# Rows of an expert's slots picked out of the resident residual by TensorE instead of gathered from DRAM

## The chip, the cores and the metric

The program runs on one core of a Trainium2 chip. A core has five engines, each with its own instruction stream: TensorE (PE, with a separate queue of weight loads, PEld), VectorE (DVE), ScalarE (ACT), GpSimd (POOL) and SyncE (SP, which here only issues DMAs). Sixteen DMA engines move data between DRAM and the on-chip memories SBUF (128 partitions) and PSUM (8 banks, written by TensorE). Engines wait for each other and for DMAs on semaphores.

The metric is the device time of one execution in microseconds; lower is better.

## The reference

One decoder layer on 264 tokens (256 of a prompt, 8 of a sample) with D_MODEL 2048, all in float32: token mixing, a mixture of experts, a gated per-layer embedding, a final norm. The change lies in the mixture of experts:

```python
x = x + hier_moe(rmsnorm(x, g_ffn), w_router_g, ..., w_gate, w_up, w_down)

# hier_moe: top-1 of 4 groups, then top-2 of the group's 8 experts; 32 experts of width 512
g_idx = argmax(g_logits); top_l, top_i = top_k(e_logits[g_idx], 2)
expert = g_idx * 8 + top_i
# rows sorted by expert, and for each expert e, with xb its tokens' rows of rmsnorm(x):
(silu(xb @ w_gate[e]) * (xb @ w_up[e])) @ w_down[e]
# the rows go back to their tokens, times their weights
```

Each of the three weights of an expert is 4 MB, so the experts read 32 x 12 MB, about 403 MB, from DRAM.

## The kernel before

**Stages.** The kernel projects, runs attention and the mLSTM, projects out, routes (`route`), runs the experts (`experts`) and ends in `tail_stage`. Each engine's stream is written out by hand; the order inside an engine is the order of the code.

**Tokens.** The residual after token mixing stays in SBUF in `x_res` [128, 3, 2048]: tokens lie on partitions, in three tiles (`TILES`) of 128, 128 and 8 tokens.

**Slots.** Every expert has 32 slots (`SLOTS`), one per token that chose it (more tokens would cause a second pass, `body(p)` with p > 0, which these inputs don't run). `route` computes which token has which rank in its expert: `rank` [128, 6], then `hot` [128, 6, 32], a one-hot row of the slot for each token (six: two choices times three tiles). `choice` holds for each token and expert the token's row number. TensorE multiplies them (`slot_table`, 24 matmuls in bank 4), and `slot_index` turns the table into row indices `idx` with an index out of bounds for an empty slot.

**Layout of an expert's input.** A row of 2048 is cut into four quarters of 512. Partition 32a + s of the tile `xe` [128, 512] holds quarter a of slot s.

**How `xe` was filled.** ACT multiplied all rows by 1/rms (`L1530`) and wrote them to a DRAM tensor `ffn_rows` by three DMAs (`L1532`). POOL gathered from it with an indirect DMA of 128 rows of 2 KB (`gather_rows`, L1905): the first with `first_rows`, the later ones, one per expert, with the index column copied to `gi` (L1899). The gather for expert e + 1 was issued after the matmuls of `x_turn` for expert e had read `xe`. The last one (column 32) has only indices out of bounds. After the expert POOL scatters the results `yq` to `expert_rows` with another indirect DMA of 128 rows (L1914).

**An expert on TensorE** (`expert`, L1852): two halves of the gate product and two of the up product (`project`, 8 matmuls each, L1827), a fold of the gate (`folded(0)`) between the two up halves, the fold of the up product, the down product in two halves (L1847), and `x_turn` (L1807), which turns `xe` of the next expert; DVE copies it to `xT` (`x_copy`, L1762). In the first four experts (`PEELED`) the products of `ple_project` follow.

**Weights.** They come in chunks of 2 MB: gate, up and down of an expert are two each. Six chunks fit in the ring (`raw` and `more`). SP issues the next chunk into a place as soon as TensorE has used the old one (`chunk_used`, L1683). In the routing stage SP loads the six chunks of expert 0 (L1418), and the two gate chunks of expert 1 into other free memory (`extra`, L1448). Those waited until the first gather had landed. Then SP waits for `xs_clear` from POOL (two memsets that follow the first gather, L1929 and L1930), issues four small loads (L1722), loads the flag of a second pass (L1665), and begins the ring.

Of the kernel before, what the change touches and what calls it, by code (L numbers as in the profile page):

```python
# [22 lines left out]
F32 = mybir.dt.float32  # L23
# [1246 lines left out]
def one_hot(core, dve, rt, shared, rank):  # L1270

    core.nc.vector.tensor_tensor(rt["hot"][:], rt["slot"][:].rearrange("p (o s) -> p o s", o=1).to_broadcast([P, 6, SLOTS]),
                                 rank.rearrange("p (m o) -> p m o", o=1).to_broadcast([P, 6, SLOTS]), ALU.is_equal
                                 ).then_inc(shared["hot_ready"], 1)


def slot_index(core, dve, rt, shared, p):
# [7 lines left out]
    if isinstance(p, int):  # L1285
        V.tensor_tensor(rt["first_rows"][:], rt["wide"][:, 0, 0:1], rt["none"][:, 0, 0:1], ALU.add)
# [36 lines left out]
def route(core, w, part, mixT, rt, rows, shared, ctx):  # L1323
# [30 lines left out]
    shifted = slice(32, 32 + NS)  # L1354
    sample_rows = core.x_res[shifted, 2, :]
    extra = [[oT[:].rearrange("p k t -> p (k t)")[:, 0:4096]], [core.gain_row[:], space[:, 0:2048]]]
    names = ("r_xT r_added r_ss r_wr_clear r_wr_landed r_wr r_br r_pin r_wp r_const r_squared r_turned r_taken r_taken1 r_logits "
             "r_l_copied r_folded r_mean r_root r_scale r_scaled r_pin_turned r_pin_copied r_in1 r_in2 r_exp1 r_exp2 "
# [4 lines left out]

    def turned_rows(t):

        return part[:].rearrange("p k t -> p (k t)").rearrange("p (g c) -> p g c", g=4)[:, :, t * GW:(t + 1) * GW]

    def pool(pool):
# [35 lines left out]
        link(G.memset(rt["xe"][:], 0.0))  # L1404
# [10 lines left out]
    def sync(sp):  # L1415
# [27 lines left out]
        sp.wait_ge(shared["gathered"], 16)  # L1443
# [6 lines left out]
    def tensor(pe):  # L1450
# [48 lines left out]
        pe.wait_ge(q["r_taken"], 8)  # L1499
        slot_table(core, pe, rt, shared, 0)  # L1500
# [3 lines left out]
    def scalar(act):  # L1504
        link = chain(act, core.act_chain)
        act.wait_ge(q["r_ss"], 1)
        for g in range(4):
# [5 lines left out]
            if g == 3:  # L1513
# [6 lines left out]
                act.wait_ge(q["r_scale"], 1)  # L1520
# [3 lines left out]
        act.wait_ge(q["r_taken"], 8)  # L1524
        act.wait_ge(q["r_taken1"], 4)
        for m, t in enumerate((1, 0, 2)):
            t0, n = TILES[t]
            xn = turned_rows(t) if t < 2 else sample_rows.rearrange("p (g c) -> p g c", g=4)
            src = core.x_res[0:n, t, :].rearrange("p (g c) -> p g c", g=4)
# [6 lines left out]
        nc.scalar.activation(c[:, 5, :], c[:, 5, :], ACT.Exp).then_inc(q["r_exp2"], 1)  # L1536
        act.wait_ge(q["r_wts"], 1)
        nc.scalar.activation(tail["wts"][:], ps[:, 7, 0:2], ACT.Copy)

    def vector(dve):  # L1540
# [29 lines left out]
        V.tensor_copy(r[shifted, 2:3], r[0:NS, 2:3]).then_inc(q["r_scale"], 1)  # L1570
# [30 lines left out]
        for n in range(2):  # L1601
            link(V.tensor_tensor(rt["choice"][:, :, :, n], six, ids[:, :, n:n + 1].to_broadcast([P, 6, NE]), ALU.mult))
# [4 lines left out]
        one_hot(core, dve, rt, shared, rt["rank"][:])  # L1607
# [5 lines left out]
        slot_index(core, dve, rt, shared, 0)  # L1613
# [10 lines left out]
    return {"pool": pool, "sync": sync, "tensor": tensor, "scalar": scalar, "vector": vector, "extra": extra, "wp_landed": q["r_wp"],  # L1624
# [18 lines left out]
def experts(core, w, rt, rows, ydram, routing, last, q, ctx):  # L1643
# [8 lines left out]
    gi, si = S("gi", [P, 1], I32), S("si", [P, 1], I32)  # L1652
    first_rows = rt["first_rows"]
    landed = core.expert_landed
    rows4 = rows.rearrange("t (a c) -> (t a) c", a=4)
# [21 lines left out]
    with nc.Block() as block:  # L1677
# [52 lines left out]
        def _(act):  # L1730
            def expert(e, n):
# [23 lines left out]
        def _(dve):  # L1755
# [10 lines left out]
            def body(p):  # L1766

                if not isinstance(p, int):
# [4 lines left out]
                    one_hot(core, dve, rt, q, moved[:])  # L1773
                    slot_index(core, dve, rt, q, p)
                else:
                    dve.wait_ge(q["gain_landed"], 16)
                x_copy(p * (NE + 1))
                with dve.Fori(0, NE) as e:
                    n = p * NE + e

# [17 lines left out]
        def _(pe):  # L1798
            def x_turn(ix):

                pe.wait_ge(q["gathered"], ix * 16 + 16)
# [50 lines left out]
            def expert(p, e, n):  # L1852
# [11 lines left out]
            def body(p):  # L1864
# [25 lines left out]
        def _(pool):  # L1890
# [5 lines left out]
            def gather(column, ix):  # L1896

                wait(q["x_turned"], ix + 1)
                nc.gpsimd.tensor_copy(gi[:], idx[:, column, 0]).then_inc(q["gather_idx"], 1)  # L1899
# [450 lines left out]
```

## Time and profile before

| | |
|---|---|
| median of 3 runs | 1666.58 us (1666.31 to 1667.29) |
| profiled execution, its own time | 1664.91 us |
| its span, first to last instruction | 1663.1 us |
| experts, from the first weights used to the last product | 550.9 to 1505.8 us |
| tail behind it | to 1663.1 us |
| PE busy | 1360.3 us, 82% |
| DVE, ACT, POOL busy | 17%, 13%, 7% |
| DMA | 542.19 MB, mean 326 GB/s |

One execution was profiled. A timeline row gives start, duration, engine, line, operation, output<-input and the number of instructions in it, then in brackets how long the engine had been idle before it and who ended that. TensorE's float32 matmul appears as two records, so 8 matmuls are "x16". A chunk's landing shows where a row of TensorE ends an idle time with a DMA as releaser: it starts within 0.1 us of the landing. A granted clock of 1.0 is 2.4 GHz, of 0.5 is 1.2 GHz.

### The profile page before, as it was taken

What the parts mean: (1) busy time and instruction counts of PE and PEld (TensorE: products, weight loads), DVE (VectorE), ACT (ScalarE), POOL (GpSimd) and SP (SyncE); (2) the same over time, 40 slices, a digit from 0 to 9 for tenths busy, and PEclk for the clock granted to TensorE, in tenths of its full rate; (3) what the DMA queues carried; (4) which work ended last, traced back from release to release, by engine and by line L of the source; (5) the groups of instructions that cost most, each with busy time, mean ns of one, the idle gap of its engine ahead of it and who ended that gap; (6) DMA issues with size and microseconds to landing.
All of it is one profiled execution on the core that took longest, in us unless ns stands there. A gap on an engine that the chain in (4) does not pass through costs nothing.

```text
span 1663.1 us, 20312 instructions
## 1 busy us (share of the span) xinstructions
PE 1360.3 (82%) x8279; PEld 757.6 (46%) x8280; DVE 275.9 (17%) x754; ACT 213.4 (13%) x482; POOL 118.4 (7%) x225
## 2 busy tenths in 40 slices
PE   9999999999998797767766767767767777776997
PEld 7878888888886332222222222222222222223543
DVE  4312221246513100000000000000000000002312
ACT  3101221223203110000000000000000000002303
POOL 1000000200050110010010000100100100100000
PEclk9999999999998887787787776777777767767999
DMA  9555333579786899999999999999999999996352
GB/s 308 184 175 183 118 126 120 196 263 323 258 331 250 351 427 427 427 427 428 428 427 428 428 426 425 418 422 422 413 420 418 419 422 421 413 390 221 102 170 85
DMA packets 110082, 542.19 MB, mean 326 GB/s; under 512 B 15579, under 2 KB 38303, under 8 KB 83648
## 3 DMA queue, kind: packets, MB, share of 16 engines
q1 hardware_dynamic: 101584, 530.56, 80.4%
q0 software_dynamic: 5200, 8.67, 1.4%
q10 hardware_dynamic: 3248, 2.26, 0.5%
q8 instruction: 36, 0.59, 0.1%
q14 instruction: 14, 0.11, 0.0%
HBM read 522.97 MB, written 26.78 MB: 331 GB/s over the span
## 4 chain that ended last, share of the span: by engine, by line
DMA 50%; PE 20%; ACT 1%; DVE 0%; issue 0%; ACTq 0%; SPq 0%; POOLq 0%; DVEq 0%
DMA raw<-in_w_up 36%; DMA more<-in_w_down 12%; PE ps L2068 7%; PE ps L1827 5%; PE ps L154 3%; PE ps L1847 2%; DMA more<-in_w_up 1%; PE ps L2085 1%; DMA more<-expert_rows 0%; PE ps L1836 0%; DMA expert_rows<-hT,si 0%; PE ps L1459 0%; PE ps L1807 0%; PE ps L2057 0%; PE ps L1469 0%
## 5 line engine op out<-in xcount | busy, mean ns | idle before, releaser
L1827 PE MATMUL ps<-raw,hT 128*32 128x512 f32 x1504 | 250.8, 800 | 191.4 <-DMA raw<-in_w_gate 90.2
L154 PE MATMUL ps<-hT,raw 128*128 128x264 f32 x1280 | 292.4, 388 | 0.0
L154 PEld LDWEIGHTS ps<-hT,raw 128*128 128x128 f32 x1280 | 241.5, 191 | 42.3 <-issue 1.7
L1827 PEld LDWEIGHTS ps<-raw,hT 128*32 128x32 f32 x1504 | 46.7, 126 | 350.9 <-DMA raw<-in_w_gate 139.3
L1847 PE MATMUL ps<-more,hid 128*32 128x512 f32 x1024 | 167.9, 787 | 29.9 <-DVE hid L1786 22.7
L154 PE MATMUL ps<-mixT,raw 128*128 128x264 f32 x640 | 145.4, 387 | 2.4 <-PEq L839 1.5
L1836 PEld LDWEIGHTS ps<-fold,hT 128*128 128x128 f32 x512 | 85.8, 251 | 120.2 <-ACT hT L1740 72.9
L154 PEld LDWEIGHTS ps<-mixT,raw 128*128 128x128 f32 x640 | 120.8, 190 | 25.0 <-issue 3.9
L1783 DVE TENSOR_TENSOR hid<-ps,sig 128x128 f32<-128x128 f32 x32 | 9.3, 292 | 671.2 <-PE ps L1836 671.2
L1827 PE MATMUL ps<-more,hT 128*32 128x512 f32 x512 | 108.4, 996 | 10.6 <-DMA more<-in_w_up 10.6
L2068 PE MATMUL ps<-raw,more 128*128 128x512 f32 x256 | 113.0, 598 | 0.0
L1836 PE MATMUL ps<-fold,hT 128*128 128x32 f32 x512 | 93.5, 335 | 23.2 <-ACT hT L1740 23.2
L1847 PEld LDWEIGHTS ps<-more,hid 128*32 128x32 f32 x1024 | 30.9, 126 | 141.4 <-DMA more<-in_w_down 59.4
L1734 ACT ACTIVATE hT<-ps 128x512 f32<-128x512 f32 x32 | 19.1, 597 | 524.6 <-PE ps L1827 524.6
L1914 POOL DMA_INDIRECT expert_rows<-hT,si x32 | 32.9, 1028 | 685.8 <-DVE hT L1791 685.8
L1807 PEld LDWEIGHTS ps<-ident,xe 128*64 128x64 f32 x1056 | 66.2, 216 | 30.8 <-issue 30.8
L2068 PEld LDWEIGHTS ps<-raw,more 128*128 128x128 f32 x256 | 48.3, 192 | 57.1 <-issue 57.1
L1807 PE MATMUL ps<-ident,xe 128*64 128x64 f32 x1056 | 70.8, 288 | 3.9 <-DMA xe<-ffn_rows,first_rows 3.9
L1791 DVE COPY hT<-ps 128x512 f32<-128x512 f32 x32 | 22.1, 692 | 182.3 <-PE ps L1847 182.3
L1827 PEld LDWEIGHTS ps<-more,hT 128*32 128x32 f32 x512 | 18.7, 154 | 53.2 <-issue 40.0
L1737 ACT ACTIVATE sig<-ps 128x128 f32<-128x128 f32 x32 | 8.9, 278 | 213.8 <-PE ps L1836 213.8
L1905 POOL DMA_INDIRECT xe<-ffn_rows,gi x32 | 33.5, 1048 | 27.3 <-POOL gi L1899 27.3
(390 smaller groups left out, 762.5 us busy)
## 6 DMA issues: line engine op xcount, KB each, us to landing
more<-in_w_down SPq DMA_DIRECT2D x64, 2048.0 KB, 26.3
raw<-in_w_gate SPq DMA_DIRECT2D x62, 2048.0 KB, 27.8
more<-in_w_up SPq DMA_DIRECT2D x32, 2048.0 KB, 26.6
raw<-in_w_up SPq DMA_DIRECT2D x32, 2048.0 KB, 27.0
raw<-in_w_in SPq DMA_DIRECT2D x44, 1024.0 KB, 5.0
raw<-in_w_out SPq DMA_DIRECT2D x16, 1024.0 KB, 8.6
raw<-in_w_ple_gate SPq DMA_DIRECT2D x16, 1024.0 KB, 5.1
x_res<-in_state_mlstm_C SPq DMA_DIRECT2D x8, 1024.0 KB, 8.5
```

The source lines that it names most:

```text
L154: return nc.tensor.matmul(ps[:, j, 0:NT], core.raw[:, q % NCH, k * GW + j * P:k * GW + (j + 1) * P], xT[:, core.groups[g].k0 + c * CK + k, ...
L1734: nc.scalar.activation(gu[:, 0, :], ps[:, GATE, :], ACT.Copy).then_inc(q["gu_copied"], 1)
L1783: V.tensor_tensor(hid[:], ps[:, GB, 0:4 * SLOTS].rearrange("p (k s) -> p k s", k=4), sig[:], ALU.mult).then_inc(q["h_step"], 1)
L1791: V.tensor_copy(yq[:], ps[:, YB, :]).then_inc(q["y_copied"], 1)
L1807: last = nc.tensor.matmul(ps[h * 64:(h + 1) * 64, XB, k * 64:(k + 1) * 64], by_row[:, k, :], quarters[:, h], start=True, stop=True)
L1827: last = nc.tensor.matmul(ps[own, (GATE, UP)[m], :], xT[:, k, i * SLOTS:(i + 1) * SLOTS], weights, start=(i == 0 and k < 4), stop=(i == EI ...
L1836: last = nc.tensor.matmul(ps[:, GB, (m * 4 + j) * SLOTS:(m * 4 + j + 1) * SLOTS], gu[:, m, :].rearrange("p (i r k) -> p i k r", i=EI, k=2) ...
L1847: last = nc.tensor.matmul(ps[a * SLOTS:(a + 1) * SLOTS, YB, :], hid[:, 2 * i + k, :], chunk(2 * EI + i)[:, k * D + a * GW:k * D + (a + 1) ...
L1905: pool.indirect_dma_start(out=xe[:], out_offset=None, in_=rows4, in_offset=bass.IndirectOffsetOnAxis(ap=which, axis=0), bounds_check=4 * N ...
L1914: pool.indirect_dma_start(out=y4, out_offset=bass.IndirectOffsetOnAxis(ap=si[:, 0:1], axis=0), in_=yq[:], in_offset=None, bounds_check=8 * ...
L2068: last = nc.tensor.matmul(ps[:, 2 * t + g % 2, :], xT[:, c * CK + k, t * P:(t + 1) * P], core.raw[:, c, k * GW:(k + 1) * GW], start=(c == ...
L2085: last = nc.tensor.matmul(ps[a * SLOTS:(a + 1) * SLOTS, 4 + g % 2, 0:P], xsT[:, k, :], core.raw[:, k // CK, k % CK * GW + a * P:k % CK * G ...
```

## The change

- `ffn_rows`, its three scaling instructions and stores on ACT, all 33 gathers and index copies on POOL, `first_rows` and `gi` are gone.
- New in SBUF: `pick_r`, the choice times 1/rms for each token and expert (column 32 is zero), `both` and `mine`.
- `pick_slots` (DVE, two instructions) makes `mine` [128, 3, 32] for one expert: `hot` times the expert's column of `pick_r`, then the sum over the two choices. `gather_slots` (TensorE, 12 matmuls of 32 columns against 512) multiplies it with `x_res` into bank 2; `slots_copy` (ACT) copies the bank to `xe`.
- For expert e + 1 this stands inside expert e: the matmuls between the second up half and the fold of the up product.
- `choice` is computed later on DVE, `slot_table` and the product of the weights move (`tables`) into expert 0, behind its gate products, and `slot_index` behind the first `x_copy`.
- SP's loads of `extra` wait for the fold of the logits and the turned `pin`, and no more for the first gather.
- POOL's two memsets still wait for `idx_ready`.

```diff
+def pick_slots(core, dve, rt, shared, ix, column):
+    V = core.nc.vector
+    V.tensor_tensor(rt["both"][:], rt["hot"][:], rt["pick_r"][:, :, column].to_broadcast([P, 6, SLOTS]), ALU.mult
+                    ).then_inc(shared["pick_step"], 1)
+    dve.wait_ge(shared["pick_step"], ix + 1)
+    V.tensor_tensor(rt["mine"][:], rt["both"][:, 0:3, :], rt["both"][:, 3:6, :], ALU.add).then_inc(shared["picked"], 1)
+
+def gather_slots(core, pe, rt, shared, ix):
+    nc, ps = core.nc, core.ps
+    pe.wait_ge(shared["picked"], ix + 1)
+    pe.sem_inc(shared["pe_tick"], 1)
+    for t, (_, n) in enumerate(TILES):
+        for a in range(4):
+            last = nc.tensor.matmul(ps[a * SLOTS:(a + 1) * SLOTS, 2, :], rt["mine"][0:n, t, :],
+                                    core.x_res[0:n, t, a * GW:(a + 1) * GW], start=(t == 0), stop=(t == 2))
+    last.then_inc(shared["x_gathered"], 1)
+
+def slots_copy(core, act, rt, shared, ix):
+    act.wait_ge(shared["x_gathered"], ix + 1)
+    core.nc.scalar.activation(rt["xe"][:], core.ps[:, 2, :], ACT.Copy).then_inc(shared["gathered"], 1)
...
     def sync(sp):
-        sp.wait_ge(shared["gathered"], 16)
+        sp.wait_ge(q["r_folded"], 1)
+        sp.wait_ge(q["r_pin_turned"], 1)
...
     def tensor(pe):
         pe.wait_ge(q["r_taken"], 8)
+        pe.wait_ge(q["r_taken1"], 4)
+        gather_slots(core, pe, rt, shared, 0)
+
+    def tables(pe):
         slot_table(core, pe, rt, shared, 0)
...
     def scalar(act):
-        for m, t in enumerate((1, 0, 2)):
...
-            nc.scalar.activation(xn, src, ACT.Copy, scale=r[0:n, t:t + 1]).then_inc(q["r_scaled"], 1)
-            act.wait_ge(q["r_scaled"], m + 1)
-            act.dma_start(rows[t0:t0 + n, :].rearrange("t (g c) -> t g c", g=4), xn).then_inc(shared["rows_stored"], 16)
+        slots_copy(core, act, rt, shared, 0)
         act.wait_ge(q["r_in1"], 1)
...
# experts, TensorE
             def expert(p, e, n):
                 project(0, 0, n)
                 project(0, 1, n)
+                if isinstance(e, int) and e == 0:
+                    routing["tables"](pe)
                 project(1, 0, n)
                 folded(0, n)
                 project(1, 1, n)
+                gather_slots(core, pe, rt, q, p * (NE + 1) + e + 1)
                 folded(1, n)
...
# experts, POOL
                 if isinstance(p, int):
-                    pool.wait_ge(q["rows_stored"], 48)
-                    pool.sem_inc(q["gather_idx"], 1)
+                    link = chain(pool, core.pool_chain)
                     pool.wait_ge(q["idx_ready"], 1)
-                    gather_rows(first_rows[:, 0:1])
...
                 with pool.Fori(0, NE) as e:
                     n = p * NE + e
-                    gather(bass.ds(e + 1, 1), p * (NE + 1) + e + 1)
                     wait(q["y_stored"], n * 16)
                     scatter(bass.ds(e, 1), n)
```

TensorE, from the end of the routing through expert 0 (the product of ranks, the table, `x_turn`, the projections), before and then after:

```order
203 L1497 MATMUL ps<-before,ones 128x96
204 L1265 MATMUL ps<-choice,hot 32x64 x24
205 L1502 MATMUL ps<-wt_tok,slot_spread 128x2
206 L1665 TENSOR_LOAD flag
207 L1665 ISA x2
208 L1807 MATMUL ps<-ident,xe 64x64 x16
209 L1827 MATMUL ps<-raw,hT 32x512 x24
210 L1836 MATMUL ps<-fold,hT 128x32 x4
211 L1827 MATMUL ps<-more,hT 32x512 x8
212 L1836 MATMUL ps<-fold,hT 128x32 x4
```

```order
203 L1516 MATMUL ps<-before,ones 128x96
204 L1292 MATMUL ps<-x_res,mine 32x512 x12
205 L1681 TENSOR_LOAD flag
206 L1681 ISA x2
207 L1832 MATMUL ps<-ident,xe 64x64 x16
208 L1852 MATMUL ps<-raw,hT 32x512 x16
209 L1265 MATMUL ps<-choice,hot 32x64 x24
210 L1525 MATMUL ps<-wt_tok,slot_spread 128x2
211 L1852 MATMUL ps<-raw,hT 32x512 x8
212 L1861 MATMUL ps<-fold,hT 128x32 x4
213 L1852 MATMUL ps<-more,hT 32x512 x8
214 L1292 MATMUL ps<-x_res,mine 32x512 x12
```

The table moved behind 16 of the 24 first projections, and twelve new matmuls stand ahead of `x_turn` and again ahead of the fold of the up product.

POOL, from its load of the flag into the loop over experts, before and then after:

```order
86 L1665 TENSOR_LOAD flag
87 L1665 ISA x2
88 L1905 DMA xe<-ffn_rows,first_rows 128x512
89 L1929 MEMSET hT 128x512
90 L1930 MEMSET hT 128x1024
91 L1932 UNCONDITIONAL_BRANCH
92 L1932 ISA
93 L1899 ISA
94 L1899 COPY gi<-idx 128x1
95 L1905 DMA xe<-ffn_rows,gi 128x512
```

```order
86 L1681 TENSOR_LOAD flag
87 L1681 ISA x2
88 L1938 MEMSET hT 128x512
89 L1939 MEMSET hT 128x1024
90 L1943 UNCONDITIONAL_BRANCH
91 L1943 ISA
92 L1927 ISA
93 L1927 COPY si<-idx 128x1
```

The gathers and their index copies are gone; the memsets stand where the first gather did.

## Rows read from the trace of the kernel before

**Rows 1.** The page's 40 slices of the span: DMA's busy share in tenths
```profile
DMA  9555333579786899999999999999999999996352
```

**Rows 2.** The chain of waits that ended last, shares of the span by line
```profile
DMA raw<-in_w_up 36%; DMA more<-in_w_down 12%; PE ps L2068 7%; PE ps L1827 5%; PE ps L154 3%; PE ps L1847 2%; DMA more<-in_w_up 1%; PE ps L2085 1%; DMA more<-expert_rows 0%; PE ps L1836 0%; DMA expert_rows<-hT,si 0%; PE ps L1459 0%; PE ps L1807 0%; PE ps L2057 0%; PE ps L1469 0%
```

**Rows 3.** Timeline of PE over one expert's period: chunks used as they land
```profile
680.18 1.92 PE L1827 MATMUL ps<-raw,hT 128*32 128x512 f32 x16 [0.89 <-DMA raw<-in_w_gate]
685.54 3.52 PE L1827 MATMUL ps<-raw,hT 128*32 128x512 f32 x16 [3.44 <-DMA raw<-in_w_gate]
691.24 2.72 PE L1827 MATMUL ps<-raw,hT 128*32 128x512 f32 x16 [2.18 <-DMA raw<-in_w_up]
...
696.14 3.34 PE L1827 MATMUL ps<-more,hT 128*32 128x512 f32 x16 [0.33 <-DMA more<-in_w_up]
...
705.93 1.92 PE L1847 MATMUL ps<-more,hid 128*32 128x512 f32 x16 [0.60 <-DMA more<-in_w_down]
```

**Rows 4.** Timeline of SP: when one place of the ring was loaded again
```profile
822.25 0.33 SPq L1683 DMA_DIRECT2D more<-in_w_up  x1
852.93 0.33 SPq L1683 DMA_DIRECT2D more<-in_w_up  x1
...
914.54 0.33 SPq L1683 DMA_DIRECT2D more<-in_w_up  x1
945.23 0.33 SPq L1683 DMA_DIRECT2D more<-in_w_up  x1
```

**Rows 5.** DMA queue of POOL, 832.3:863 and 924.4:955.1: packets, MB, share of engines
```profile
q0 software_dynamic: 160, 0.38, 3.1%
...
q0 software_dynamic: 160, 0.22, 2.0%
```

**Rows 6.** Timeline of PE in the last two experts
```profile
1452.55 2.86 PE L1827 MATMUL ps<-raw,hT 128*32 128x512 f32 x16 [2.99 <-DMA raw<-in_w_gate]
1458.39 3.64 PE L1827 MATMUL ps<-raw,hT 128*32 128x512 f32 x16 [2.98 <-DMA raw<-in_w_up]
...
1483.18 2.77 PE L1827 MATMUL ps<-raw,hT 128*32 128x512 f32 x16 [2.94 <-DMA raw<-in_w_gate]
1488.45 3.64 PE L1827 MATMUL ps<-raw,hT 128*32 128x512 f32 x16 [2.50 <-DMA raw<-in_w_up]
...
1503.15 2.62 PE L1847 MATMUL ps<-more,hid 128*32 128x512 f32 x16 [0.49 <-DMA more<-in_w_down]
```

**Rows 7.** Timeline of POOL: the gather of column 32
```profile
1479.19 1.05 POOL L1905 DMA_INDIRECT xe<-ffn_rows,gi  x1 [0.85 <-POOL gi L1899]
```

**Rows 8.** Timelines of DVE, ACT, POOL and PE where the experts begin
```profile
538.41 0.36 DVE L1272 TENSOR_TENSOR hot<-slot,rank 128x192 f32<-128x192 f32 x1
...
542.04 0.17 DVE L1615 TENSOR_REDUCE rc<-ra 128x3 f32<-128x12 f32 x1 [0.81 <-ACT ra L1534]
...
540.50 1.28 ACT L1534 ACT_TABLE_LOAD   x1 [0.36 <-ACT x_res L1530]
...
545.96 0.95 POOL L1930 MEMSET hT<- 128x1024 f32 x1
...
547.80 2.22 PE L1807 MATMUL ps<-ident,xe 128*64 128x64 f32 x32 [3.88 <-DMA xe<-ffn_rows,first_rows]
550.88 7.72 PE L1827 MATMUL ps<-raw,hT 128*32 128x512 f32 x48 [0.85 <-DVE hT L1762]
```

**Rows 9.** Timeline of SP where the experts begin
```profile
547.69 0.33 SPq L1448 DMA_DIRECT2D oT<-in_w_gate  x1
...
549.01 3.00 SPq L1722 DMA_DIRECT2D hT<-x_res  x4
```

**Rows 10.** Loads of the flag (line 1665), ns min/median/max, and their start
```profile
L1665 DVEq TENSOR_LOAD <-flag x1: 543/543/543, 543.4 to 543.4; - x1
...
L1665 SPq TENSOR_LOAD <-flag x1: 809/809/809, 552.1 to 552.1; - x1
```

**Rows 11.** Timeline of PE: the second up chunk of expert 1
```profile
582.30 3.01 PE L1827 MATMUL ps<-more,hT 128*32 128x512 f32 x16 [2.10 <-DMA more<-in_w_up]
```

More of the change, by code:

```diff
@@ L1320, in ple_copy, with route @@
         nc.scalar.activation(dst, src, ACT.Copy).then_inc(shared["pp_copied"], 1)
-def route(core, w, part, mixT, rt, rows, shared, ctx):
+def route(core, w, part, mixT, rt, shared, ctx):
     nc, ps = core.nc, core.ps
@@ L1536, in scalar, with after @@
         nc.scalar.activation(c[:, 5, :], c[:, 5, :], ACT.Exp).then_inc(q["r_exp2"], 1)
+    def after(act):
         act.wait_ge(q["r_wts"], 1)
@@ L1600, in vector @@
         six = pick[:].rearrange("p i t e -> p (i t) e")
-        for n in range(2):
-            link(V.tensor_tensor(rt["choice"][:, :, :, n], six, ids[:, :, n:n + 1].to_broadcast([P, 6, NE]), ALU.mult))
+        link(V.tensor_tensor(rt["pick_r"][:, :, 0:NE].rearrange("p (i t) e -> p i t e", i=2), pick[:],
+                             r[:].rearrange("p (o t u) -> p o t u", o=1, u=1).to_broadcast([P, 2, 3, NE]), ALU.mult))
         dve.wait_ge(q["r_ranked"], 1)
@@ L1612, in vector @@
                         ).then_inc(shared["flag_ready"], 1)
-        slot_index(core, dve, rt, shared, 0)
+        for n in range(2):
+            link(V.tensor_tensor(rt["choice"][:, :, :, n], six, ids[:, :, n:n + 1].to_broadcast([P, 6, NE]), ALU.mult))
+        dve.sem_inc(shared["hot_ready"], 1)
         dve.wait_ge(q["r_exp1"], 1)
@@ L1640, in ring_slot, with experts @@
     return part.rearrange("p a c -> p (a c)")
-def experts(core, w, rt, rows, ydram, routing, last, q, ctx):
+def experts(core, w, rt, ydram, routing, last, q, ctx):
     nc, ps = core.nc, core.ps
@@ L1772, in body @@
                     dve.wait_ge(q["rank_moved"], p)
-                    one_hot(core, dve, rt, q, moved[:])
+                    one_hot(core, dve, rt, q, moved[:]).then_inc(q["hot_ready"], 1)
                     slot_index(core, dve, rt, q, p)
+                    pick_slots(core, dve, rt, q, p * (NE + 1), slice(0, 1))
                 else:
@@ L1894, in wait @@
                 pool.sem_inc(q["pool_tick"], 1)
-            def gather(column, ix):
-                wait(q["x_turned"], ix + 1)
-                nc.gpsimd.tensor_copy(gi[:], idx[:, column, 0]).then_inc(q["gather_idx"], 1)
-                wait(q["gather_idx"], ix + 1)
-                gather_rows(gi[:, 0:1])
-            def gather_rows(which):
-                pool.indirect_dma_start(out=xe[:], out_offset=None, in_=rows4,
-                                        in_offset=bass.IndirectOffsetOnAxis(ap=which, axis=0),
-                                        bounds_check=4 * NT - 1, oob_is_err=False).then_inc(q["gathered"], 16)
             def scatter(column, iy):
@@ L1919, in body @@
                 if isinstance(p, int):
-                    pool.wait_ge(q["rows_stored"], 48)
-                    pool.sem_inc(q["gather_idx"], 1)
+                    link = chain(pool, core.pool_chain)
                     pool.wait_ge(q["idx_ready"], 1)
-                    gather_rows(first_rows[:, 0:1])
-                else:
-                    wait(q["idx_ready"], p + 1)
-                    gather(slice(0, 1), p * (NE + 1))
-                if isinstance(p, int):
-                    link = chain(pool, core.pool_chain)
                     link(nc.gpsimd.memset(tail["xs"], 0.0))
```

62 lines of the change are left out of this document (29 added, 33 removed).

## The prediction

> **What bounds the kernel now.** I read the page's slices first. From the fifteenth slice to the thirty-fifth the DMA engines are busy all the time [rows 1], and the chain of waits lies on the loads of the experts' weights: 36% and 12% of the span [rows 2]. TensorE is busy too, but the timeline shows it waiting for nearly every chunk [rows 3]. So between about 550 and 1503 us the time is the transfer time of a stream, and a step on another engine is paid only if it stops the stream, at its beginning or behind its end.
>
> The pace of the stream comes next. The rows of TensorE show chunks being used as they land. The second up chunk to the second down chunk, two chunks later, is 9.79 us; the second up chunk follows the first by 4.90 us: 4.90 us for a bare 2 MB chunk. Two intervals of the period are longer, 5.36 and 5.70 us [rows 3], and in them lie POOL's scatter and gather. Six bare chunks are 29.4 us; the period is 30.68 and 30.69 us [rows 4]. So both indirect DMAs together cost about 1.27 us per expert.
>
> How is that split? The queue of POOL moved 0.38 MB in one such period and 0.22 MB in another, since experts have different numbers of tokens [rows 5]. The two periods do not differ by more than 0.01 us [rows 4]. The mean of valid bytes is therefore not what counts. A reading that fits: each DMA engine serves fixed slots, a chunk has landed only when its last engine is done, and the engine with the low, always filled slots carries 8 rows of 16 KB in all in every gather and every scatter. At its share of a chunk (2 MB / 16 = 128 KB in 4.90 us) 16 KB takes 0.61 us, and twice that is 1.22 us, near the 1.27.
>
> The last gather is a test of it, as all its indices are out of bounds [rows 7]. The first up chunk of the last expert came 30.06 us after that of the expert before (1488.45 less 1458.39), while the second gate chunk came after 30.63 us (1483.18 less 1452.55) [rows 6]. So the gather without rows gave back 0.57 us. I take 0.61 us per gather; the bounds are 0.57 us and 0.66 us (the rest of the period over bare chunks, 30.69 less 29.37, halved).
>
> The Trainium skill, page "DMA: Bandwidth & Descriptors", section "The descriptor swizzle", has engine 0 write partitions 0 to 3 and 32 to 35 of a 128-partition transfer, and so on in fours. By that rule two engines would serve slots 0 to 3 alone, the reading above; no row here shows single engines. By the mean of bytes the removal would be worth half (rival A).
>
> **The stream without the gathers.** Gathers that run while the stream is closed up behind expert 1's second up chunk are those for experts 3 to 31, 29 of them; the two earlier ones lie in the start, below, and the last moved nothing. 29 x 0.61 = 17.7 us less (16.5 to 19.1). The stores of `ffn_rows` and the first gather lie ahead of the stream.
>
> **The start.** Today SP issues the extra chunks at 547.69, right after the first gather, four small loads from 549.01 for 3.00 us [rows 9], and goes on to the ring; the second up chunk of expert 1 is used at 582.30, after a wait for the DMA [rows 11]. From there the stream is closed. When does that chunk land now?
>
> The extra chunks are issued some 16 us earlier, once the logits are folded and `pin` is turned. That gains nothing by itself, for SP then waits for `xs_clear`, which comes from POOL behind `idx_ready`, and the table for it moved into expert 0. Step by step:
> - `hot` starts at 538.41 and takes 0.36 [rows 8]; `pick_slots` adds two such instructions, 0.39 and 0.26. `picked` is at 539.5. `pick_r` takes the place of `choice`, at no cost.
> - The 12 matmuls are 24 records in the form of a projection, three rounds of four. 16 such records take 1.92 us at the full clock [rows 3] and 3.64 at half [rows 6], so 24 take 2.8 or 5.4. The projections at 550.88 still began at half clock, as their 7.72 us for 48 records show (5.8 at full, 10.9 at half) [rows 8], so I count half here: until 544.9. ACT's copy (0.6, as its other copies of 512 columns) ends at 545.5.
> - `x_turn` takes 2.2 [rows 8] and would be done at 547.8. But ACT has the copy ahead of its exponentials now: a table load of 1.28, and DVE's next step follows 1.54 us after the table load's start (542.04 less 540.50) [rows 8], so at 547.1. From there DVE needs 1.9 us to its load of the flag's end (its load starts at 543.4 and takes 0.54 [rows 10], 1.36 + 0.54 after 542.04) and 0.3 us of register work. `x_copy` starts at 549.3 and takes 0.7, and the first projection is at 550.05 instead of 550.88 [rows 8]: 0.8 us earlier only.
> - Two gate chunks: 3.8 us at full clock, 7.3 at half. By the 7.72 us before, the clock rose some 4 us into the projections, which would make 5.8 for two chunks; with more work ahead of them now I take 5.5. Then the table 1.5, `slot_index` 0.8, POOL's memsets (0.95 [rows 8] and a shorter one) 1.6, the four small loads 3.0 [rows 9], SP's load of the flag 0.81 and some register work, 1.2 [rows 10]. SP reaches the ring at 550.05 + 13.6 = 563.7 (562.0 to 565.4).
> - Gate chunks of expert 2 and both up chunks of expert 1 are then free to be issued together. Four chunks are 19.6 us, the scatter of expert 0 is 0.6, and first byte and small loads are 2.0 to 3.4. (Before: six chunks and three row DMAs, 31.2 us, of 34.6 between 547.69 and 582.30 [rows 9, 11].) The chunk lands at 563.7 + 22.8 = 586.5, against 582.30: 4.2 us later (1.9 to 6.7).
>
> So the start costs time: the DMA engines stand idle from the end of the extra chunks, near 546, to 563.7.
>
> **TensorE inside the stream.** 2.8 to 5.4 us are added per expert, and about 0.7 are hidden in the wait for ACT's copy of the up product, which the matmuls now fill. In the period of 1452.55 the waits for DMA are 2.99 and 2.98 [rows 6], so TensorE needs 24.7 of 30.69 us; with the addition 26.8 to 29.4, against 30.08. Being late by up to 5 us frees places in the ring late, but five chunks of 4.90 us are queued. DVE's two instructions run while TensorE projects, and ACT's copy while it folds: nothing. POOL loses work nobody waits for.
>
> **Behind the end.** The last expert runs the matmuls as well, for column 32, which is zero. The last down chunk was waited for by only 0.49 us [rows 6], so nearly all of the addition is paid: 2.8 to 5.4 less 0.7 and 0.5 gives 1.6 to 4.2; where the filled wait keeps the clock up for the down products, part comes back. I take 2 (0 to 5). The tail is as before.
>
> **Sum.** -17.7 + 4.2 + 2 = -11.5 us. The profiled execution took 1664.91 us itself (span 1663.1), 1.7 below the median: 1653.4 by it, 1655.1 by the median of 1666.58. The terms' ends give -17.2 to -4.8, that is 1649 to 1662.
>
> **Rival A: the gather cost only its bytes.** Row bytes of both DMAs are 0.22 to 0.38 MB; half of the middle, 0.15 MB at 2 MB per 4.90 us, is 0.35 us. 29 x 0.35 = 10.2, and with the start and the end 4 us are left: 1662.6. For it speaks only that the queue's share of the engines' time is 2 to 3% [rows 5]; against it the constant period and the last gather.
>
> The same skill page, section "Measured", has time grow with size up to 425 GB/s, which for the bytes alone is this rival.
>
> **Rival B, slower: TensorE becomes the bound.** If the throttle holds it at half clock for most of the period, four projections take 14.6, two folds 3.8, the down product 7.2, `x_turn` 2.1, hand-overs 1.6 and the new matmuls 5.4: 34.7 us. That is 4.0 above 30.69: 29 x 4.0 = 116 us, and with start and end 1789. It decides from the point at which TensorE needs more than 30.08 us, 0.7 above my upper estimate, and the kernel is slower by over 0.2% from 30.6. Against it: a TensorE that is late no longer waits, and where it did not wait its clock was 1.0. I hold a small part for it, and with it for matmuls that do not run four at a time.
>
> **Rival C: the whole excess was the gather's.** Then the period falls to 29.4: 29 x 1.27 = 36.8, 1636. The last gather speaks against it: without its rows the period was still 30.06, 0.7 above bare chunks, and the scatter was there.
>
> **How the numbers follow.** Forecast 79%, A 9%, B 6%, C 3%, the rest (a start that differs from the steps by over 5 us) 3%. The forecast's terms reach 1649 to 1662; I give 1648 to 1662.5, which takes in half of A. A difference of 0.2%, 3.3 us, is about what can be told from none. Faster by more: nearly all of the forecast, half of A and C, 86%. Within: 7%. Slower: 7%.
>
> **What would show it.** The period of the ring: 30.1 us right, 30.3 A, 29.4 C, over 30.7 with no waits for DMA on TensorE B. SP's first ring load at 562 to 565.4, idle DMA engines ahead of it, and the second up chunk of expert 1 at 584 to 589. The last product 2.7 to 7.7 us after the last landing (2.67 before). I am wrong if SP isn't held by `xs_clear`, or if scatters grow dearer without the gathers beside them.

## The result and the profile after

The changed kernel took 1650.19 us (median of 5 runs, 1649.27 to 1656.24), against 1666.33 us (5 runs) for the kernel before on the same chip: a ratio of 0.9912, 95% interval 0.9894 to 0.9931, so 11.5 to 17.7 us less. The forecast was 1655.0 us, 1648.0 to 1662.5. The profiled execution took 1652.54 us, with a span of 1650.5 us and a mean granted clock of 0.916 (before: 1664.91, 1663.1, 0.849).

The page of the changed kernel: the slices of TensorE's clock and the DMA share, the queue of POOL, the chain by line, and the groups of the new matmuls and of the down products. They answer [rows 1] and [rows 2].

```profile
PEclk9999999999999799888888898888987978987999
DMA  9555333578886599999999999999999999996252
...
q0 software_dynamic: 2560, 4.34, 0.7%
...
DMA raw<-in_w_up 47%; PE ps L2078 7%; PE ps L1852 6%; PE ps L154 4%; DMA more<-in_w_down 2%; PE ps L2095 1%; PE ps L1292 1%; PE ps L1872 1%; DMA more<-expert_rows 0%; DMA expert_rows<-hT,si 0%; PE ps L1478 0%; PE ps L1861 0%; PE ps L2067 0%; PE ps L1488 0%; PE ps L1324 0%
...
L1872 PE MATMUL ps<-more,hid 128*32 128x512 f32 x1024 | 127.8, 629 | 41.7 <-DVE hid L1811 22.7
...
L1292 PE MATMUL ps<-x_res,mine 128*32 128x512 f32 (+1 forms) x792 | 101.8, 628 | 2.2 <-DVE mine L1282 2.2
```

The stream still fills the middle, and the slices just ahead of it are now less busy. The chain still lies on the loads. The new matmuls keep TensorE busy for 101.8 us, and only 1% of the chain is theirs.

Timeline of PE of the changed kernel in one period and in the last two experts; it answers [rows 3] and [rows 6].

```profile
690.87 3.58 PE L1852 MATMUL ps<-raw,hT 128*32 128x512 f32 x16 [3.44 <-DMA raw<-in_w_gate]
695.88 1.92 PE L1852 MATMUL ps<-raw,hT 128*32 128x512 f32 x16 [1.42 <-DMA raw<-in_w_up]
700.77 3.24 PE L1852 MATMUL ps<-more,hT 128*32 128x512 f32 x16 [1.91 <-DMA more<-in_w_up]
...
1440.03 1.92 PE L1852 MATMUL ps<-raw,hT 128*32 128x512 f32 x16 [3.46 <-DMA raw<-in_w_gate]
...
1464.62 1.92 PE L1852 MATMUL ps<-raw,hT 128*32 128x512 f32 x16 [0.89 <-DMA raw<-in_w_gate]
1470.00 3.64 PE L1852 MATMUL ps<-raw,hT 128*32 128x512 f32 x16 [3.46 <-DMA raw<-in_w_gate]
1475.01 3.64 PE L1852 MATMUL ps<-raw,hT 128*32 128x512 f32 x16 [1.37 <-DMA raw<-in_w_up]
...
1481.76 2.89 PE L1292 MATMUL ps<-x_res,mine 128*32 128x512 f32 x24
...
1489.78 1.89 PE L1872 MATMUL ps<-more,hid 128*32 128x512 f32 x16
```

The period is 29.97 us (1470.00 less 1440.03; over 26 periods, 1470.00 less 690.87, it is 29.967), against 30.68 in [rows 4]. The second gate chunk to the first up chunk is 5.01 us, where it was 5.70 [rows 3]. The second up chunk follows after 4.89. The interval from the first to the second gate chunk stays long, 5.38 us (1464.62 to 1470.00) where it was 5.36; I take it that most of the scatter lies in it.

The two periods of [rows 4] do not stand for all of them. From first up chunk to first up chunk, from expert 4 on, the median of the kernel before is 30.64 us, and a few of its periods reach 30.8 to 31.0; those of the changed kernel all lie between 29.94 and 29.99. So most periods fell by 0.67 us, and a few by more.

Timelines of SP, POOL and PE of the changed kernel where the experts begin; they answer [rows 8], [rows 9] and [rows 11].

```profile
527.11 0.38 SPq L1459 DMA_DIRECT2D mixT<-in_w_ple_proj  x1
562.03 3.47 SPq L1738 DMA_DIRECT2D hT<-x_res  x4
566.87 0.82 SPq L1699 DMA_DIRECT2D raw<-in_w_gate  x2
...
560.41 0.53 POOL L1938 MEMSET hT<- 128x512 f32 x1 [65.87 <-DVE idx L1311]
...
541.98 5.50 PE L1292 MATMUL ps<-x_res,mine 128*32 128x512 f32 x24 [2.19 <-DVE mine L1282]
...
552.79 6.14 PE L1852 MATMUL ps<-raw,hT 128*32 128x512 f32 x32 [2.29 <-DVE hT L1783]
...
585.12 3.62 PE L1852 MATMUL ps<-raw,hT 128*32 128x512 f32 x16 [2.60 <-DMA raw<-in_w_up]
590.02 1.92 PE L1852 MATMUL ps<-more,hT 128*32 128x512 f32 x16 [0.22 <-DMA more<-in_w_up]
```

This execution was 2.2 us late before the change's first step: SP's load of `mixT` ahead of it started at 527.11, against 524.89 (524.72 in e5 below). Beyond that, SP reached the ring at 566.87, and the second up chunk of expert 1 was used at 590.02 instead of 582.30: 7.7 us later, 5.5 without the 2.2.

Windows of the changed kernel at that place. After the length come the busy times of PE, PEld, DVE, ACT and POOL with their counts, then granted clock, DMA share and GB/s.

```profile
550.00:555.00 5.00, 2.71 (x21) 0.91 (x22) 1.44 (x6) 0.00 (x0) 0.00 (x0) 0.50 0.02 3
555.00:560.00 5.00, 5.00 (x78) 1.96 (x74) 0.33 (x2) 0.06 (x1) 0.00 (x0) 0.71 0.00 0
560.00:565.00 5.00, 5.00 (x48) 2.04 (x44) 0.93 (x4) 2.43 (x5) 1.67 (x3) 1.00 0.05 10
```

The DMA engines move next to nothing for some 15 us ahead of the stream.

**The balance of the two spans.** From the second up chunk of expert 1 to the first up chunk of the last expert there were 906.15 us (582.30 to 1488.45), and there are 884.99 us (590.02 to 1475.01): 21.2 us less. The beginning is 7.7 us longer. From there to the end of the last down product is 16.66 us (to 1491.67) instead of 17.32 (to 1505.77). The tail is 158.8 us instead of 157.3. The change doesn't touch it, and in the kernels of this document it lies between 156.9 and 159.3 us whatever was changed. The sum is 7.7 - 21.2 - 0.7 + 1.5 = -12.7 us, and the spans differ by 12.6. Without the 2.2 and the tail's 1.5, the change itself is worth -16.4 us, near the difference of the medians, 16.1.

### The profile page after: what moved, and what is told of

Same layout as the page of the kernel before. It is cut to its first block, busy times and chain, and to the rows that moved or that the text cites. A ratio compares the mean times of both kernels' runs of the same rounds, so it can differ in the third digit from the quotient of the medians.

```text
span 1650.5 us, 21888 instructions
## 1 busy us (share of the span) xinstructions
PE 1361.2 (82%) x9071; PEld 759.6 (46%) x9072; DVE 293.2 (18%) x819; ACT 227.5 (14%) x512; POOL 75.4 (5%) x160
## 3 DMA queue, kind: packets, MB, share of 16 engines
q0 software_dynamic: 2560, 4.34, 0.7%
## 4 chain that ended last, share of the span: by engine, by line
DMA 50%; PE 20%; DVE 1%; issue 0%; ACT 0%; DVEq 0%; SPq 0%; POOLq 0%; ACTq 0%
DMA raw<-in_w_up 47%; PE ps L2078 7%; PE ps L1852 6%; PE ps L154 4%; DMA more<-in_w_down 2%; PE ps L2095 1%; PE ps L1292 1%; PE ps L1872 1%; DMA more<-expert_rows 0%; DMA expert_rows<-hT,si 0%; PE ps L1478 0%; PE ps L1861 0%; PE ps L2067 0%; PE ps L1488 0%; PE ps L1324 0%
## 5 line engine op out<-in xcount | busy, mean ns | idle before, releaser
L1852 PE MATMUL ps<-raw,hT 128*32 128x512 f32 x1504 | 241.9, 776 | 177.7 <-DMA raw<-in_w_gate 107.8
L1872 PE MATMUL ps<-more,hid 128*32 128x512 f32 x1024 | 127.8, 629 | 41.7 <-DVE hid L1811 22.7
L1292 PE MATMUL ps<-x_res,mine 128*32 128x512 f32 (+1 forms) x792 | 101.8, 628 | 2.2 <-DVE mine L1282 2.2
L1852 PE MATMUL ps<-more,hT 128*32 128x512 f32 x512 | 79.9, 753 | 26.0 <-DMA more<-in_w_up 25.9
L1861 PEld LDWEIGHTS ps<-fold,hT 128*128 128x128 f32 x512 | 68.6, 205 | 67.4 <-issue 67.4
L1861 PE MATMUL ps<-fold,hT 128*128 128x32 f32 x512 | 75.7, 293 | 0.0
L1292 PEld LDWEIGHTS ps<-x_res,mine 128*32 128x32 f32 (+1 forms) x792 | 24.1, 117 | 82.1 <-issue 82.1
```

The costliest lines, as they stand in the source:

```text
L1292: last = nc.tensor.matmul(ps[a * SLOTS:(a + 1) * SLOTS, 2, :], rt["mine"][0:n, t, :], core.x_res[0:n, t, a * GW:(a + 1) * GW], start=(t == ...
L1852: last = nc.tensor.matmul(ps[own, (GATE, UP)[m], :], xT[:, k, i * SLOTS:(i + 1) * SLOTS], weights, start=(i == 0 and k < 4), stop=(i == EI ...
L1861: last = nc.tensor.matmul(ps[:, GB, (m * 4 + j) * SLOTS:(m * 4 + j + 1) * SLOTS], gu[:, m, :].rearrange("p (i r k) -> p i k r", i=EI, k=2) ...
L1872: last = nc.tensor.matmul(ps[a * SLOTS:(a + 1) * SLOTS, YB, :], hid[:, 2 * i + k, :], chunk(2 * EI + i)[:, k * D + a * GW:k * D + (a + 1) ...
```

## Experiments

Chips differ. On the chips of the experiments the kernel before took 1668.91 us (one run, beside e1 to e4), 1668.28 us (median, beside e5 to e8) and 1672.29 us (median, beside e9 and e10). Of e1 to e4 and e9 there is one run each, the profiled one, so their times have no interval. For the cost of a gather I therefore use the traces: the time from the first up chunk of expert 1 to the first up chunk of the last expert, 30 periods. TensorE waited for the DMA at both ends in all the kernels of this table (1475.01 less 585.12 for the changed kernel).

**An unread gather put back on POOL (e1 to e4, e9).** In the changed kernel POOL gathers rows of `w_out` into a scratch tile once per expert, behind `x_turn`'s signal and ahead of the scatter's wait. The kernels differ in the indices, and in a few small instructions ahead of the stream that make them. The edit, shortened:

```diff
+ wait(q["x_turned"], n + 2)
+ wait(q["dummy_done"], n * 16)
+ nc.gpsimd.tensor_copy(rt["gi"][:], INDEX).then_inc(q["dummy_idx"], 1)
...
+ pool.indirect_dma_start(out=rt["junk"][:], out_offset=None, in_=w_rows,
...
  wait(q["y_stored"], n * 16)
  scatter(bass.ds(e, 1), n)
# INDEX: e1 idx[:, e + 1, 0] (the real rows); e2 idx[:, NE, 0] (none valid);
# e3 8 times the partition (all 128 rows); e4 the same for even partitions only;
# e9 the same for partitions 0 to 15 of every 32 only
```

> The kernel after, with a gather put back that nobody needs: once per expert POOL copies the same index column as before and gathers 128 rows of 2 KB (from the first 2 MB of w_out instead of ffn_rows, into a scratch tile that no one reads). Both theories: the period of the stream, 29.97 us after, goes back to 30.68, so 0.71 us per expert. If it stays near 30.0, the period fell for another reason than the gather.

> As the gather put back, but every index is out of bounds, so no row is moved. If an empty gather costs the rest that the last gather of before left (0.71 less 0.57), the period is 29.97 + 0.14 = 30.11 us. If an empty gather is free: 29.97.

> As the gather put back, but all 128 indices are valid, twice the rows that an expert's gather has on average. Theory slowest engine (a DMA engine serves fixed partitions, the one with the always filled slots sets the landing): the same as with real indices, 30.68 us. Rival bytes: the part for rows doubles, 0.14 + 2 x 0.57 = 1.28 us, period 31.25 us.

> As the gather put back, but the even partitions have valid indices and the odd ones are out of bounds: 64 rows, about as many as an expert has on average, spread evenly over all groups of partitions. Theory slowest engine: each engine has half of its rows, 0.14 + 0.57 / 2 = 0.43 us, period 30.40 us. Rival bytes: 64 rows cost as the real ones, 30.66 us.

> The changed kernel with one unread row gather per expert on POOL, as in e3 and e4, but of slots 0 to 15 of every group of 32 (64 rows; the other 64 are out of bounds). It moves the bytes of e4 (64 rows), but those 64 rows are neighbours and not every other one. Theory (fixed slots of neighbours to each DMA engine, the slowest engine sets the landing): the period is that of e3 with all 128 rows, 30.65 us, and the time is 1668 to 1671 us. Rival (the bytes of the transfer count): the period is that of e4, 30.34 us, and the time is 1660 to 1663 us.

| Kernel | Time, us | 30 periods, us | per gather | median period, us | POOL's queue, MB |
|---|---|---|---|---|---|
| changed | 1650.19 | 889.89 | | 29.97 | 4.34 |
| e2, no rows | 1651.13 | 891.62 | 0.06 | 30.04 | 4.35 |
| e4, every other row | 1662.36 | 900.55 | 0.36 | 30.34 | 8.54 |
| e3, all rows | 1670.22 | 910.53 | 0.69 | 30.66 | 12.73 |
| e1, the real rows | 1673.67 | 912.09 | 0.74 | 30.65 | 8.53 |
| e9, the low half | 1673.37 | 913.41 | 0.78 | 30.67 | 8.54 |

"Per gather" is the excess of the 30 periods over the changed kernel, divided by 30. In e1 the last of the 30 gathers is that of column 32, without rows; the other 29 cost 0.76 us each.

Timelines of PE at the first up chunks of expert 1 and of the last expert, of e2, e4, e3, e1 and e9, in that order.

```profile
581.25 1.92 PE L1854 MATMUL ps<-raw,hT 128*32 128x512 f32 x16 [3.09 <-DMA raw<-in_w_up]
...
1472.87 1.92 PE L1854 MATMUL ps<-raw,hT 128*32 128x512 f32 x16 [1.62 <-DMA raw<-in_w_up]
```
```profile
583.28 1.92 PE L1859 MATMUL ps<-raw,hT 128*32 128x512 f32 x16 [3.47 <-DMA raw<-in_w_up]
...
1483.83 3.64 PE L1859 MATMUL ps<-raw,hT 128*32 128x512 f32 x16 [2.40 <-DMA raw<-in_w_up]
```
```profile
582.66 3.27 PE L1856 MATMUL ps<-raw,hT 128*32 128x512 f32 x16 [3.12 <-DMA raw<-in_w_up]
...
1493.19 3.64 PE L1856 MATMUL ps<-raw,hT 128*32 128x512 f32 x16 [2.06 <-DMA raw<-in_w_up]
```
```profile
584.54 3.45 PE L1854 MATMUL ps<-raw,hT 128*32 128x512 f32 x16 [2.99 <-DMA raw<-in_w_up]
...
1496.63 3.64 PE L1854 MATMUL ps<-raw,hT 128*32 128x512 f32 x16 [2.39 <-DMA raw<-in_w_up]
```
```profile
582.79 3.64 PE L1861 MATMUL ps<-raw,hT 128*32 128x512 f32 x16 [3.09 <-DMA raw<-in_w_up]
...
1249.24 3.64 PE L1861 MATMUL ps<-raw,hT 128*32 128x512 f32 x16 [2.84 <-DMA raw<-in_w_up]
1280.21 3.64 PE L1861 MATMUL ps<-raw,hT 128*32 128x512 f32 x16 [2.98 <-DMA raw<-in_w_up]
...
1496.20 3.20 PE L1861 MATMUL ps<-raw,hT 128*32 128x512 f32 x16 [2.43 <-DMA raw<-in_w_up]
```

What follows. e4, e1 and e9 move the same bytes, and the gather costs 0.36, 0.76 and 0.78 us: bytes do not set the price, and where the valid rows lie does. The low half of each group costs no less than all rows. That is what fixed slots of neighbours for each engine give, with the slowest engine ending the transfer. The rivals that count bytes expected 31.25 us for the period of e3 and 30.34 for that of e9; the medians are 30.66 and 30.67. No row shows single engines, though. The other reading, that the rows of e9 lie badly in DRAM, is not tested by itself; the real rows of e1 lie elsewhere in `w_out` and have the same median.

An empty gather costs 0.06 us, where e2 was expected to show 0.14 or nothing. So the rows themselves cost 0.30 for every other one (0.31 by 8 KB of 128 KB in 4.90 us) and 0.63 for all (0.61 by 16 KB).

By the medians of the single periods e1, e3 and e9 cost the same, 0.68, 0.69 and 0.70 us. The further 0.07 to 0.10 us of e1 and e9 in the mean lie in a few long periods. In e9 the one shown is 30.97 us (1280.21 less 1249.24); 9 of the 26 periods that its timeline lets one read are over 30.75, the longest 31.19. In e1 it is 7 of 28, up to 31.01, and in e3 none, the longest 30.74. The DMA engines are busy all through the long periods too (share 1.00), but move 415 to 419 GB/s, where they move 420 and 421 in the last two periods, and TensorE's granted clock is lower, 0.77 to 0.81 against 0.88 and 0.89. What makes them longer stays open.

The DMA view shows the difference in the bandwidth. Stretch 1300 to 1400 us of e3, then of e9: packets and MB in all, and the mean.

```profile
DMA packets 3465, 42.73 MB, mean 427 GB/s; under 512 B 562, under 2 KB 562, under 8 KB 954
```
```profile
DMA packets 3384, 41.75 MB, mean 418 GB/s; under 512 B 654, under 2 KB 654, under 8 KB 895
```

With all rows the gathers cost time because they move bytes: the total stays at 427 GB/s. With the low half the total falls to 418 GB/s, which fits engines that carry no rows and lose time while others carry theirs. The real gathers of e1 give 417 GB/s, those of the kernel before 422.

**The matmuls twice (e10).** In the loop over experts the 12 matmuls are done twice, the second time over the first.

```diff
-    for t, (_, n) in enumerate(TILES):
+    for t, (_, n) in times * list(enumerate(TILES)):
...
- gather_slots(core, pe, rt, q, p * (NE + 1) + e + 1)
+ gather_slots(core, pe, rt, q, p * (NE + 1) + e + 1, 2)
```

> The changed kernel with the 12 matmuls of each gather inside the loop over experts done twice, the second time over the first, 2.9 us more of TensorE per expert at the full clock. Theory (TensorE has that slack behind the stream): the period stays 29.97 us, and only the start (the doubled matmuls of experts 0 and 1) and the end (2.9 us for the last expert) can pay: 1652 to 1658 us. Rival (TensorE is as long as the stream already): the period grows, and each 0.1 us of it costs 2.9 us; by 2.9 us per expert it would be 1734 us.

It took 1651.98 us (1648.77 to 1653.41, 4 runs); ratio to before on that chip 0.9885, interval 0.9858 to 0.9912. Timeline of PE of e10 at one expert and at the last.

```profile
693.75 3.64 PE L1852 MATMUL ps<-raw,hT 128*32 128x512 f32 x16 [3.56 <-DMA raw<-in_w_up]
...
1467.39 1.92 PE L1852 MATMUL ps<-raw,hT 128*32 128x512 f32 x16 [0.18 <-DMA raw<-in_w_gate]
1473.00 2.66 PE L1852 MATMUL ps<-raw,hT 128*32 128x512 f32 x16 [3.68 <-DMA raw<-in_w_up]
...
1481.08 5.73 PE L1292 MATMUL ps<-x_res,mine 128*32 128x512 f32 x48
...
1488.57 3.64 PE L1872 MATMUL ps<-more,hid 128*32 128x512 f32 x32 [0.71 <-DVE hid L1811]
```

The period is (1473.00 less 693.75) / 26 = 29.971 us, unchanged. The wait for the second gate chunk has shrunk from 3.46 us to 0.18, but TensorE still waits 3.68 us for the first up chunk. That is more than another set of matmuls takes at the full clock (2.89). Only behind the last landing do they show: 19.2 us from the first up chunk to the last product (1473.00 to 1492.21) instead of 16.7. The time lies at the low end of what was expected.

**The matmuls behind the down product (e8).**

```diff
  project(1, 1, n)
- gather_slots(core, pe, rt, q, p * (NE + 1) + e + 1)
  folded(1, n)
  down(n)
+ gather_slots(core, pe, rt, q, p * (NE + 1) + e + 1)
```

> The kernel after, with the twelve matmuls behind the down product instead of ahead of the fold of the up product. TensorE then waits for ACT's copy of the bank (0.6 us and two semaphores) ahead of x_turn in each expert. Theory (TensorE has slack in every period, only start and end are paid): the period stays 29.97, and the last product comes 2 to 3 us earlier, as the last expert's matmuls stand behind it: 1647 to 1650. Rival (the place counts in every period, since it delays the release of the ring's places or fills ACT's wait): the period is longer by up to 1 us, 1650 to 1680.

It took 1651.04 us (1646.99 to 1659.06, 6 runs), ratio 0.9907 (0.9878 to 0.9936); the changed kernel has 0.9912. Timeline of PE of e8 in the last periods and at its end.

```profile
1447.34 2.96 PE L1852 MATMUL ps<-raw,hT 128*32 128x512 f32 x16 [3.07 <-DMA raw<-in_w_up]
...
1477.30 1.92 PE L1852 MATMUL ps<-raw,hT 128*32 128x512 f32 x16 [0.74 <-DMA raw<-in_w_up]
...
1491.97 2.13 PE L1872 MATMUL ps<-more,hid 128*32 128x512 f32 x16 [0.56 <-DMA more<-in_w_down]
...
1508.25 1.11 PE L2067 MATMUL ps<-ident,x_res 128*128 128x128 f32 x4 [8.42 <-DVE x_res L2210]
```

The period is 29.96, and the last product ends 16.8 us after the first up chunk, where it was 16.7. I had expected it 2 to 3 us earlier, and that missed: ahead of the last down product the matmuls had cost nothing that moving them could give back. Behind it TensorE waits 8.4 us for the last rows anyway, so the last expert's matmuls are hidden there too. In time the two places can't be told apart.

**The scratch rows cleared early (e5), and the exponentials first as well (e6).** In e5 POOL clears `xs` and `ybs` ahead of its wait for the index table, and SP waits instead for ACT's last copy of the residual (`taken`), which also guards the buffer. In e6 ACT's copy of the gathered slots also stands behind the two exponentials of the routing.

```diff
# e5 and e6, POOL
- pool.wait_ge(q["idx_ready"], 1)
  link(nc.gpsimd.memset(tail["xs"], 0.0))
  link(nc.gpsimd.memset(tail["ybs"], 0.0))
  pool.sem_inc(q["xs_clear"], 1)
+ pool.wait_ge(q["idx_ready"], 1)
# e5 and e6, SP
  sp.wait_ge(q["xs_clear"], 1)
+ sp.wait_ge(routing["taken"], 8)
# e6 alone, ACT
- slots_copy(core, act, rt, shared, 0)
  act.wait_ge(q["r_in1"], 1)
  nc.scalar.activation(a[:], a[:], ACT.Exp).then_inc(q["r_exp1"], 1)
  act.wait_ge(q["r_in2"], 1)
  nc.scalar.activation(c[:, 5, :], c[:, 5, :], ACT.Exp).then_inc(q["r_exp2"], 1)
+ slots_copy(core, act, rt, shared, 0)
```

> The kernel after, with POOL's two memsets ahead of its wait for idx_ready; SP, which no longer has that wait in its way, waits for ACT's last copy of the residual instead. Theory (the start of the stream is held by xs_clear): SP's first load of the ring moves from 566.9 to the first use of a gate chunk, about 556 us, its fourth from 568 to about 565, the second up chunk of expert 1 lands at 579 to 582 instead of 590.0, and the time falls by 8 to 11 us to about 1641. Rival (the stream begins when TensorE has used chunks, whatever SP waits for): within 2 us of after.

> As the early memsets, and ACT takes its two exponentials, with their table load, ahead of the first copy of the gathered rows. DVE then has its weights done before x_turn ends: the first projection starts 1.5 to 2 us earlier than in the kernel after (552.8). Both theories: another 1.5 to 2 us less than with the early memsets alone, about 1639.

e5 took 1639.84 us (1639.62 to 1640.75, 4 runs), ratio 0.9843 (0.9826 to 0.9861). e6 took 1637.78 us (1637.02 to 1642.12, 4 runs), ratio 0.9838 (0.9818 to 0.9859). Timelines of SP and PE of e5.

```profile
524.72 0.38 SPq L1459 DMA_DIRECT2D mixT<-in_w_ple_proj  x1
...
554.11 3.02 SPq L1699 DMA_DIRECT2D raw<-in_w_gate  x2
...
1462.48 1.92 PE L1853 MATMUL ps<-raw,hT 128*32 128x512 f32 x16 [1.67 <-DMA raw<-in_w_up]
```

Counted from SP's load of `mixT` (524.72 and 527.11), SP reaches the ring 10.4 us earlier than in the changed kernel, and the first up chunk of the last expert is used 10.1 us earlier; the medians, of two chips, differ by 10.4, and by the ratios to the kernel before it is 11.5. So the cost of the start was the wait of `xs_clear`, as the prediction had it. In e6 the ring is reached another 2.4 us earlier.

```profile
524.33 0.38 SPq L1459 DMA_DIRECT2D mixT<-in_w_ple_proj  x1
551.33 2.89 SPq L1699 DMA_DIRECT2D raw<-in_w_gate  x2
```

Those are SP's rows of e6. Its median is 2.1 us below e5's, about the 1.5 to 2 expected, but the intervals overlap: e6 isn't shown to be faster than e5. Both are faster than the changed kernel and than the one before.

**The kernel before with the extra chunks issued early (e7).** The other half of the change's start alone.

```diff
- sp.wait_ge(shared["gathered"], 16)
+ sp.wait_ge(q["r_folded"], 1)
+ sp.wait_ge(q["r_pin_turned"], 1)
```

> The kernel before, with one edit of the change alone: SP's extra chunks wait for the folded logits and the turned pin instead of the first gather. xs_clear comes at 547 there, so SP is held only until the first gate chunk is used, 554.6. Four chunks then follow, of which the last lands near 578 instead of 582.3: 3 to 5 us faster than before, 1662 to 1663. If early extra chunks gained nothing anywhere: 1666.

That missed: 1673.8 us (1672.5 to 1682.2, 5 runs), ratio 1.0052 (1.0024 to 1.008), slower where 3 to 5 us of gain were expected. Timelines of ACT and POOL of e7 and its windows, then the same gather in the kernel before.

```profile
541.50 0.30 ACTq L1533 DMA_DIRECT2D ffn_rows<-x_res  x1
...
555.82 1.26 POOL L1906 DMA_INDIRECT xe<-ffn_rows,first_rows  x1 [61.91 <-issue]
```
```profile
545.00:550.00 5.00, 0.25 (x2) 0.16 (x1) 0.00 (x0) 0.17 (x1) 0.00 (x0) 0.50 0.99 374
...
555.00:560.00 5.00, 0.55 (x10) 0.58 (x10) 0.00 (x0) 0.00 (x0) 2.75 (x3) 0.50 0.11 28
```
```profile
544.09 1.26 POOL L1905 DMA_INDIRECT xe<-ffn_rows,first_rows  x1 [51.37 <-DMA ffn_rows<-x_res]
```

The extra chunks now lie on the DMA engines together with the stores of `ffn_rows`. The first gather reads `ffn_rows` and waits in the code until its three stores have landed (`rows_stored`): it starts 14.3 us behind the issue of the last store, where it was 3.9 (540.17 to 544.09 in the kernel before). So the first projection moves back by some 10 us (562.51 instead of 550.88, in an execution that was 1.3 us late by then), and the DMA engines are nearly idle from 555 on. The chunks that have been loaded by then give only part of it back. In the changed kernel the stores and that gather are gone, and no row of TensorE there waits for a DMA between the early issue and the first projection.

## Why the prediction was right, point by point

- **The direction and the path**: right. The loads stay the bound, and the time goes with the period.
- **The price of a gather**: mis-sized. I took 0.61 us, with 0.66 as the upper bound; the stream gave back 21.2 us over 29 gathers, 0.73 each. The step that failed is the test by the last gather. I read its 0.57 us as the price of a gather, but that gather was still issued, and e2 prices an empty one at 0.06. The upper bound failed with it: I halved the excess over six bare chunks, and without the gather only 0.57 of it is left to the scatter (29.97 less 29.40). And I read the two periods of [rows 4] as all of them: the median gather costs 0.67, just above my bound, and the rest up to 0.73 lies in a few longer periods.
- **The slowest engine**: supported by e3, e4 and e9, and by the bandwidth. No row shows single engines, and the long periods of the uneven gathers have no explanation here. The Trainium skill, page "DMA: Bandwidth & Descriptors", section "The descriptor swizzle", has engine 0 of a 128-partition transfer write partitions 0 to 3 and 32 to 35, and so on in fours. By that rule slots 0 to 15 of each group would lie on 8 engines of 16 with 8 rows each, and every other slot on all engines with 4 rows each. This case's 0.78 against 0.36 us agrees with it.
- **The start**: the steps held, the size was a little low, 5.5 us instead of 4.2 and inside its bounds. Less the 2.2 us of this execution, the gather's matmuls began at 539.8 (539.5 predicted) and took 5.50 at half clock (5.4), the first projection began at 550.6 (550.05), SP reached the ring at 564.7 (563.7) and the chunk was used at 587.8 (586.5). The small loads took 3.47, not 3.0. That `xs_clear` holds SP is shown by e5.
- **The end**: wrong in sign, -0.7 instead of +2. I let nearly all of the matmuls be paid behind the last landing. But the last product follows the landing of the last down chunk, three chunks of 4.90 us after the first up chunk (1475.01 and 14.7 make 1489.7; the weight loads of the last 16 products end a wait of 1.34 us for that chunk at 1489.67). The matmuls fit ahead of it: the down product began 11.41 us behind the first up chunk (1486.42), where it was 11.61 before (1500.06). The last 16 products then ran in 1.89 us instead of the 2.62 of [rows 6]. e10 shows where the room ends: with twice the matmuls, 2.5 us are paid. e8 gained nothing by moving them.
- **TensorE in the stream**: right. The matmuls take 2.89 us there, the full clock, near the lower of the two ends I had kept. The mean clock rose from 0.849 to 0.916, and the mean matmul record of the down products fell from 787 to 629 ns. e1, with the matmuls and a gather, has 0.887 and 595 ns, so the shorter period alone isn't what raised the clock. The place of the matmuls counts for the down products: behind them, in e8, the mean is 819 ns at a clock of 0.893. e10's clock is 0.926.
- **Rival A** (bytes only) falls by the period, 29.97 and not 30.3, and by e4 against e9. **Rival B** (TensorE as the bound) falls by e10: no period longer, with twice the work added. **Rival C** (the whole excess was the gather's) falls by the period too, 29.97 and not 29.4.
- **The sum**: the stream's 3.5 us more and the end's 2.7 us, against 1.3 us more at the start, make -16.4 of my -11.5. Stream and end both lie outside the bounds that I had given them, on the same side. That the total is still inside the range is in part luck: the dearer start took back some of it.

## What to carry to other kernels

A small indirect DMA beside a saturated stream was priced here by where its valid rows lie and not by its bytes, as if by its fullest DMA engine: spread the valid rows over all the slots, or take the rows from a resident copy if the engine that would do it waits anyway. When work moves in a start-up sequence, follow each waiting queue to what it really needs; here a clearing of scratch rows, placed behind a wait it had no use for, held the load queue and was worth 10 us. Before a load is issued earlier, look for small transfers beside it that others wait for: in e7 they cost more than the early load gave.

## What I had not expected of the hardware

- A gather of half of the rows, crowded in the low slots (e9), costs 0.78 us in the mean, no less than all of the rows, 0.69; the same number spread evenly costs 0.36. The total bandwidth is 418, 427 and 428 GB/s.
- With uneven gathers (before, e1, e9) a few periods are 0.35 to 0.52 us longer than the median; with all rows, every other row or none (e3, e4, e2) the longest is 0.19 us longer at most.
- A gather with no valid row costs the stream 0.06 us. POOL's queue has 5120 packets in all five kernels with the extra gather, however many rows are valid, and 2560 without it.
- 4 MB of loads issued some 3 us ahead of three row stores (e7) held back the gather that reads the stored rows by some 10 us.
- With 12 further matmuls per expert ahead of the down products the mean granted clock rose from 0.849 to 0.916, and the matmuls of the down products became 20% shorter (787 to 629 ns). Behind them (e8) the clock was 0.893 and the down products' mean 819 ns.
